# A weight ring of 24 parts instead of 23, two tiles' residual rows in PSUM, and the second tile's returned rows summed by GpSimd and VectorE

## The reference

```python
x  = x + token_mixer(rms_norm(x, norm_mix), ...)        # attention and gated linear attention
hn = rms_norm(x, norm_ffn)
g_logits = hn @ w_rg + b_rg                             # 4 groups: the best one
e_logits = hn @ w_re + b_re                             # 8 experts in a group: the best two
for each expert e:                                      # 32 experts, 1024 -> 256 -> 1024
    out += weight[:, e] * ((silu(hn @ w_gate[e]) * (hn @ w_up[e])) @ w_down[e])
return rms_norm(x + out, norm_final)
```

## Time and profile before

| | us |
|---|---|
| median of 3 runs | 604.9 (604.71 to 605.81) |
| the profiled execution | 604.58 |
| its span in the profile | 602.8 |
| TensorE busy | 574.2 (95%) |
| VectorE busy | 254.6 (42%) |
| ScalarE busy | 214.5 (36%) |
| GpSimd busy | 61.6 (10%) |
| mean of the DMAs | 259 GB/s |

### The profile page before, as it was taken

How to read it: one execution, slowest core, us unless ns; L and a number is a source line. 1 busy time by engine, 2 the same in 40 slices (tenths; PEclk the granted TensorE clock), 3 DMA queues, 4 the chain that set the end, 5 groups by cost and what they waited for, 6 DMA issues and landing times.

```text
span 602.8 us, 8673 instructions
## 1 busy us (share of the span) xinstructions
PE 574.2 (95%) x3428; PEld 434.6 (72%) x3429; DVE 254.6 (42%) x572; ACT 214.5 (36%) x438; POOL 61.6 (10%) x106
## 2 busy tenths in 40 slices
PE   7999999999999999999999998999999999877885
PEld 4978989888788888888888874766666676544342
DVE  4645677645445765533472375211211211101126
ACT  6634666555786522422152241011111111100114
POOL 3110000001000001100000011012211221111002
PEclk9999999999999999999999999999999999999898
DMA  8365130712231222198789667999999999999996
GB/s 301 87 207 177 58 111 5 291 59 71 71 104 46 61 70 71 37 342 280 291 310 414 246 252 276 380 414 425 422 421 425 424 424 421 425 425 423 425 385 277
DMA packets 59435, 156.02 MB, mean 259 GB/s; under 512 B 8368, under 2 KB 38472, under 8 KB 47744
## 3 DMA queue, kind: packets, MB, share of 16 engines
q1 hardware_dynamic: 54512, 145.74, 63.3%
q0 software_dynamic: 4864, 9.69, 4.2%
q10 hardware_dynamic: 16, 0.00, 0.0%
HBM read 147.31 MB, written 16.27 MB: 271 GB/s over the span
## 4 chain that ended last, share of the span: by engine, by line
PE 76%; DMA 11%; SPq 5%; DVE 4%; ACT 2%; issue 1%; POOL 1%; DVEq 0%; ACTq 0%; POOLq 0%
PE mid_rows L810 17%; PE last_rows L810 16%; PE bank L1247 12%; DMA slots<-expert_w_up 9%; PE bank L810 7%; PE bank L803 5%; SPq L555 5%; PE mid_rows L1267 5%; PE last_rows L868 2%; PE mid_rows L945 2%; DMA w<-w_in 1%; PE mid_rows L868 1%; PE bank L923 1%; PE bank L1118 1%; PE bank L924 1%
## 5 line engine op out<-in xcount | busy, mean ns | idle before, releaser
L1247 PE MATMUL bank<-slots,xgT 128*64 128x256 f32 x544 | 73.0, 381 | 5.2 <-DMA slot2b<-expert_w_up 1.9
L1882 DVE TENSOR_TENSOR w_low<-w,w_high 128x1024 fp32r<-128x1024 f32 x32 | 39.2, 1225 | 78.5 <-ACT w_high L1503 78.5
L1247 PEld LDWEIGHTS bank<-slots,xgT 128*64 128x64 f32 x544 | 49.2, 137 | 23.0 <-issue 4.0
L2237 DVE TENSOR_SCALAR y<-mid_rows,slot_weights 128x512 f32<-128x512 f32 x15 | 11.3, 751 | 99.7 <-PE mid_rows L1267 99.7
L1503 ACT ACTIVATE w_high<-w 128x1024 fp32r<-128x1024 f32 x32 | 33.7, 1054 | 48.6 <-PE last_rows L810 48.6
L1678 ACT ACTIVATE y<-mid_rows,slot_weights 128x512 f32<-128x512 f32 x15 | 10.3, 687 | 95.0 <-PE mid_rows L1267 70.8
L1247 PE MATMUL bank<-slot2b,xgT 128*64 128x256 f32 x240 | 36.6, 381 | 0.2 <-DMA slot2b<-expert_w_up 0.2
L1267 PE MATMUL mid_rows<-slots,hT 128*64 128x512 f32 x112 | 29.1, 594 | 2.6 <-issue 2.6
L1672 ACT ACTIVATE h_silu<-bank 128x256 f32<-128x256 f32 x15 | 5.8, 383 | 72.1 <-PE bank L1247 72.1
L1247 PEld LDWEIGHTS bank<-slot2b,xgT 128*64 128x64 f32 x240 | 23.7, 137 | 7.6 <-issue 1.6
L810 PE MATMUL mid_rows<-x_high,w_high 128*128 128x512 f32 x72 | 28.7, 398 | 0.0
(11 more groups left out here) (424 smaller groups left out, 1368.8 us busy)
## 6 DMA issues: line engine op xcount, KB each, us to landing
slots<-expert_w_up SPq DMA_DIRECT2D x18, 1024.0 KB, 24.3
slots<-expert_w_gate SPq DMA_DIRECT2D x17, 1024.0 KB, 12.8
slots<-expert_w_down SPq DMA_DIRECT2D x15, 1024.0 KB, 24.5
w<-w_in SPq DMA_DIRECT2D x16, 512.0 KB, 3.7
slot2b<-expert_w_up SPq DMA_DIRECT2D x8, 1024.0 KB, 27.2
slot2b<-expert_w_gate SPq DMA_DIRECT2D x7, 1024.0 KB, 16.7
w<-w_in SPq DMA_DIRECT2D x7, 840.0 KB, 4.6
slot2b<-expert_w_down SPq DMA_DIRECT2D x5, 1024.0 KB, 28.9
```

The source lines that it names most:

```text
L1247: ins = mm(bank[2][e * SLOTS:(e + 1) * SLOTS, m * FE:(m + 1) * FE], xgT[:, c, e * SLOTS:(e + 1) * SLOTS], weights(own, m, e, c * FE, (c + ...
L1882: V.tensor_tensor(wl2[:, u % 2, :], raw2[:, u % 2, :], wh2[:, u % 2, :].bitcast(F32), ALU.subtract).then_inc(s["lo_done"], 1)
L2237: V.tensor_scalar(y_sb[:, 512:1024], bank[5][:, :], weight, None, ALU.mult).then_inc(s["y_outD"], 1)
```

## The change

- **Ring.** R becomes 24. The old two-piece place becomes one whole place (`slot2f`, over tiles 2 and 3 of `x2`), and `split` now has three pieces: the front of `fixed` (4 KB), 2 KB beside the hidden activations and 2 KB in `early`. `early` is one allocation that holds constants and small tables that nobody needs once `act_done` is set. Part 23, the first that lies there, is issued after the halved parts (now 24 and 25) and after a wait for `act_done`. Four parts are loaded in three DMAs (before: four in two).
- **Room for it.** `h_silu` and `h_sb` become one buffer, multiplied in place; `slot_weights`, `by_pair` and `last_tokens` lie elsewhere.
- **PSUM.** Tile 2's rows stay in `mid_rows` from the residual to the end, as tile 3's do in `last_rows`. So nothing else may use banks 4 and 5: the turned rows of tiles 2 and 3 go to banks 0, 2 and 3, 0, the rank and count products to banks 2 and 3, and the down products to banks 0 and 1. `turn_x` writes these too and now waits for `y_outA` and `y_outD`. The last pair's gathered rows are turned into banks 2 and 3.
- **Tail.** ScalarE's copies of `x2` into `mid_rows` are gone. Tile 1's two returned rows are loaded beside each other, added by GpSimd, and the sum is added to `x2` by VectorE before the two accumulations of tile 1; TensorE's four products for them are gone. All eight products of the last pair now stand ahead of the returned rows' products.

```diff
-        TURNED = ((0, 1), (2, 3), (4, 5), (3, 5))
+        TURNED = ((0, 1), (2, 3), (0, 2), (3, 0))
-        LT_BANK = {0: 0, 2: 2, 3: 4}
+        LT_BANK = {0: 1, 2: 2, 3: 0}
-        split = (fixed[:, 0:PART // 2], place_at(YB + 3 * D, "slot2f", PART // 2)[:, :])
+        slot2f = place_at(YB + 2 * D, "slot2f", PART)
+        split = (fixed[:, 0:PART // 2], place_at(SMALL + 512, "slot2g", 512)[:, :], early[:, 0:512])
+        SPLIT_AT = (0, PART // 2, PART // 2 + 512, PART)
         ring = (part0 + [behind[4]] + part1 + [slot2a[:, i_ * PART:(i_ + 1) * PART] for i_ in range(2)]
-                + [behind[3]] + behind[0:3] + [slot2c[:, :], slot2d[:, :], slot2e[:, :], split])
+                + [behind[3]] + behind[0:3] + [slot2c[:, :], slot2d[:, :], slot2e[:, :], slot2f[:, :], split])
-        h_silu, h_sb = place_at(SMALL, "h_silu", FE)[:, :], place_at(SMALL + FE, "h_sb", FE)[:, :]
-        hT = v3(place_at(SMALL + 2 * FE, "hT", 2 * P), P)
+        h_silu = h_sb = place_at(SMALL, "h", FE)[:, :]
+        hT = v3(place_at(SMALL + FE, "hT", 2 * P), P)
         def rows_of(t):
-            return x2[:, t, :] if t < NT - 1 else last_rows[:, :]
-
-        def summed_rows(t):
             return (x2[:, 0, :], x2[:, 1, :], mid_rows[:, :], last_rows[:, :])[t]
...
                 if ring[q % R] is split:
-                    load_half(q, 0)
-                    load_half(q, 1)
+                    for i, piece in enumerate(split):
+                        cols = slice(SPLIT_AT[i], SPLIT_AT[i + 1])
+                        sp.dma_start(piece, (g_rows, u_rows, d_rows)[m][:, 2 * pair + e, cols]).then_inc(m_in[pair % 4][m], 16)
...
                 sp.wait_ge(s["g_done"], h + 1)
                 for e in range(2):
                     load_half(R + e, h)
+            sp.wait_ge(s["act_done"], 1)
+            load_part(23)
...
-                sp.dma_start(zt[:, t], rows.rearrange("(p w) n -> p w n", w=2) if t == 0 else
+                sp.dma_start(zt[:, t], rows.rearrange("(p w) n -> p w n", w=2) if t < 2 else
                              rows.rearrange("(i p) n -> p i n", i=2)).then_inc(s[f"rows_in{t}"], 16)
...
             pool.sem_inc(s["moe_done"], 1)
+            pool.wait_ge(s["rows_in1"], 32)
+            nc.gpsimd.tensor_tensor(zt[:, 1, 0, :], zt[:, 1, 0, :], zt[:, 1, 1, :], ALU.add).then_inc(s["row_sum"], 1)
...
             def turn_hn(t):
                 pe.wait_ge(s["hn_done"], t + 1)
                 for c in range(KC):
-                    if t == NT - 1 and c % 4 == 0:
-                        pe.wait_ge(s["hnT_outD"], 2 + c // 4)
+                    if t == 2 and c % 4 == 0:
+                        pe.wait_ge(s["hnT_outA"], 1 + c // 4)
+                    if t == 3 and c % 4 == 0:
+                        pe.wait_ge(s[("hnT_outD", "hnT_outA")[c // 4]], 2 + c // 4)
...
-            def turn_x(n, k, loads):
+            def turn_x(n, k, loads, rows_out):
                 pe.wait_ge(s[f"gathered{k}"], 16 * loads)
                 xv = xg[k].rearrange("p (q c) -> p c q", c=KC)
                 for c in range(KC):
+                    if rows_out is not None and c % 4 == 0:
+                        pe.wait_ge(s[("y_outA", "y_outD")[c // 4]], rows_out)
...
-                            ins = mm(bank[4 + f][e * SLOTS:(e + 1) * SLOTS, :], hT[:, j, e * SLOTS:(e + 1) * SLOTS],
+                            ins = mm(bank[f][e * SLOTS:(e + 1) * SLOTS, :], hT[:, j, e * SLOTS:(e + 1) * SLOTS],
...
             to_tokens(0, 0, 2, True).then_inc(s["comb_done"], 1)
-            to_tokens(0, 1, 3, True)
+            to_tokens(0, 1, 3, True).then_inc(s["comb_done"], 1)
+            to_tokens(0, 2, 4, False)
             to_tokens(0, 3, 6, False)
-            to_tokens(1, 0, 1, True).then_inc(s["comb_done"], 1)
-            to_tokens(1, 1, 0, True)
+            to_tokens(1, 0, 0, True).then_inc(s["comb_done"], 1)
+            to_tokens(1, 1, 1, True).then_inc(s["comb_done"], 1)
+            to_tokens(1, 2, 5, False)
             to_tokens(1, 3, 7, False)
-            pe.wait_ge(s["rows_in1"], 32)
-            rows_to_tokens(1, 0, 3).then_inc(s["comb_done"], 1)
-            rows_to_tokens(1, 1, 0).then_inc(s["comb_done"], 1)
-            for f in range(2):
-                pe.wait_ge(s["mid_in"], f + 1)
-                to_tokens(f, 2, 4 + f, False)
...
-            for f in range(2):
-                act.wait_ge(s["ly_lo"], f + 1)
-                A(mid_rows[:, f * 512:(f + 1) * 512], x2[:, 2, f * 512:(f + 1) * 512], ACT.Copy).then_inc(s["mid_in"], 1)
...
-                    V.tensor_tensor(x2[:, t, cols] if t < NT - 1 else bank[k][:, :], x2[:, t, cols], bank[k][:, :], ALU.add
+                    V.tensor_tensor(rows_of(t)[:, cols], x2[:, t, cols], bank[k][:, :], ALU.add
                                     ).then_inc(s["x2_done"], 1)
...
             accumulate(1, 0, 0, 2)
-            accumulate(2, 0, 1, 1)
-            accumulate(3, 1, 0, 3)
-            accumulate(4, 1, 1, 0)
+            accumulate(3, 0, 1, 0)
+            dve.wait_ge(s["row_sum"], 1)
+            dve.wait_ge(s["dve_step"], step(V.tensor_tensor(x2[:, 1, :], x2[:, 1, :], zt[:, 1, 0, :], ALU.add)))
+            accumulate(2, 1, 0, 3)
+            accumulate(4, 1, 1, 1)
```

More of the change, by code:

```diff
@@ L139, in hybrid_encoder, with early_view @@
         K = {n: cst[:, a:b] for n, (a, b) in CONST.items()}
-        rb = sb("rb", [P, NG + EXPERTS])
-        sink = sb("sink", [P, HEADS])
-        gcol = sb("gcol", [P, KC])
+        early, at_ = sb("early", [P, 540]), 0
+        def early_view(shape, words, dt=F32, rows=P):
+            nonlocal at_
+            at_ += words
+            view = early[0:rows, at_ - words:at_]
+            view = view if dt == F32 else view.bitcast(dt)
+            if len(shape) == 1:
+                return view
+            return view.rearrange("p (a b) -> p a b", b=shape[1]) if len(shape) == 2 else view
+        rb = early_view([NG + EXPERTS], NG + EXPERTS)
+        sink, gcol = early_view([HEADS], HEADS), early_view([KC], KC)
+        dec = early_view([GH, 2 * NT], 2 * GH * NT)
+        between = early_view([GH, NT - 1], GH * (NT - 1))
+        oss, ors = early_view([NT, GH], NT * GH), early_view([NT, GH], NT * GH)
+        selb = early_view([NT, EXPERTS], NT * EXPERTS // 2, BF16)
+        beforeb, onesb = early_view([P], P // 2, BF16), early_view([P], P // 2, BF16)
+        pi = early_view([5, 2 * NT], 10 * NT, I32)
+        cnt = early_view([EXPERTS + PAIRS], EXPERTS + PAIRS, F32, 1)
+        actf = early_view([116], 116, F32, 1)
+        assert 512 <= at_ <= 540
         row_norms = sb("row_norms", [P, 6, NT])
@@ L297, in hybrid_encoder @@
         ZERO_PIECES = 2 * NT
-        arrived = {(n_, m_): sum(32 if q_ in HALVED or ring[q_ % R] is split else 16 for q_, (p_, w_, _) in enumerate(order)
+        arrived = {(n_, m_): sum(16 * len(split) if ring[q_ % R] is split else 32 if q_ in HALVED else 16 for q_, (p_, w_, _) in enumerate(order)
                                  if w_ == m_ and p_ % 4 == n_ % 4 and p_ <= n_) for n_ in range(PAIRS) for m_ in range(3)}
@@ L429, in weights @@
                 return at[:, a:b]
-            return at[a // D][:, a % D:a % D + b - a]
+            piece = max(i for i in range(len(split)) if SPLIT_AT[i] <= a)
+            return at[piece][:, a - SPLIT_AT[piece]:b - SPLIT_AT[piece]]
         def down_rows(n, e, j, f):
@@ L567, in load_half @@
                 cols = slice(h * PART // 2, (h + 1) * PART // 2)
-                sp.dma_start(split[h] if ring[q % R] is split else ring[q % R][:, cols], (g_rows, u_rows, d_rows)[m][:, 2 * pair + e, cols]).then_inc(m_in[pair % 4][m], 16)
+                sp.dma_start(ring[q % R][:, cols], (g_rows, u_rows, d_rows)[m][:, 2 * pair + e, cols]).then_inc(m_in[pair % 4][m], 16)
             sp.wait_ge(s["lo_done"], LOWS)
@@ L1196, in _ @@
             for u in range(NT):
-                ins = mm(bank[4][0:1, P:P + EXPERTS], onesb[:, 0:1], selb[:, u, :], start=(u == 0), stop=(u == NT - 1),
+                ins = mm(bank[3][0:1, P:P + EXPERTS], onesb[:, 0:1], selb[:, u, :], start=(u == 0), stop=(u == NT - 1),
                          skip_group_check=True)
@@ L1831, in _ @@
             dve.wait_ge(s["const_in"], 32)
-            V.tensor_copy(beforeb[:], K["before"]).then_inc(s["cb_done"], 1)
-            V.tensor_copy(onesb[:], K["ones"]).then_inc(s["cb_done"], 1)
+            V.tensor_copy(beforeb, K["before"]).then_inc(s["cb_done"], 1)
+            V.tensor_copy(onesb, K["ones"]).then_inc(s["cb_done"], 1)
             V.tensor_copy(pair_base, K["e512"][0:1, :]).then_inc(s["cb_done"], 1)
@@ L2089, in router_out @@
                 V.tensor_tensor(lg[:, t0:t1, :], bank[1 + t0][:, t0 * (NG + EXPERTS):t1 * (NG + EXPERTS)].rearrange(
[L2090 removed]
+                    "p (t n) -> p t n", n=NG + EXPERTS), rb.unsqueeze(1).to_broadcast([P, t1 - t0, NG + EXPERTS]), ALU.add
                     ).then_inc(s["rl_out"], 1)
@@ L2161, in _ @@
```

(4 more changed lines are left out.)

62 lines of the change are left out of this document (27 added, 35 removed).

## The result

The changed kernel takes 611.65 us (median of 4, 611.41 to 612.97), the kernel before 605.07 in the same runs: a ratio of 1.0107 (95% interval 1.0089 to 1.0126). The profiled execution took 611.71 with a span of 609.9. It is slower, as forecast, but by 6.6 us instead of 3.0, and lies outside the forecast range of 604.7 to 608.9.

What follows compares the result with a forecast made beforehand. The prediction took the kernel as bound by weight DMAs, then a serial tail of 26 us. From a median of 604.9 us, 3.2 lost in the tail less 0.2 gained by the ring gave 607.9, range 604.7 to 608.9.

Steps and rivals of the forecast that it cites:

- Bound by the DMAs, then a serial tail: Expert stage: DMAs need 17.3 us a pair against TensorE's 12.0; then the last 26 us are serial.
- The ring of 24 parts: Weight prefetch, 380 to 382 us: a 24th place gains 0.2 us; ends 1.3 gained and 0.3 lost.
- The pieces, as a term of the same step: Four parts loaded in three pieces, half of each in 2 KB rows: at worst 0.3 us lost.
- Router and pair loop, nothing: Moved PSUM banks before and in the expert pairs: waits covered by 0.15 and 2.5 us, so no cost.
- The tail: After the last weights: GpSimd's 2.2 us sum delays VectorE's second addition; tile 1's squares start 3.2 us late.
- One sign: In the tail: tile 1's squares would start 2 to 3 us after tile 0's end, where they followed at once.
- the first (GpSimd misses the boundary): Tail: rows land 0.2 us later, GpSimd's sum follows VectorE's second addition; 1.9 us late, 606.6 us; chance 0.29.
- The second (no blocking): Tail: GpSimd's sum hardly delays VectorE, or takes only 1.1 us; 1.0 to 1.4 late, about 605.9; chance 0.12.
- The third (a gain of the ring): Weight prefetch: the 24th place gains 1.3 to 2.47 us; 603.4 to 604.9 us; chance 0.12.
- The fourth (the ring gives nothing, 608.1): Weight prefetch: part 23 loads too late, gaining 0, tail as forecast; 608.1 us, counted inside the main case.
- The sum: Whole kernel: 3.2 lost in the tail less 0.2 gained by the ring, added to 604.9: 607.9 us.
- the main case: Whole kernel: GpSimd's sum goes ahead of VectorE's second addition; 607.9 us, own range 606.9 to 608.9; chance 0.44.

Runs made afterwards that it cites:

- the pieces alone: Kernel before, with its four split parts loaded in three DMAs instead of two, the second half in two pieces with 2 KB rows: 605.80 us, ratio 1.0015.
- part 23 out of the way: Changed kernel with 32 bytes taken away and second tile's rows added by TensorE (605.87), part 23 issued behind part 29, 8 us later: 605.83 us, ratio 1.0007.
- where it was made to happen: Changed kernel with 32 bytes taken away (608.69), GpSimd's sum made to wait until both VectorE additions are done: 607.75 us, ratio 1.0033.

## Why the prediction was wrong, step by step

- **Bound by the DMAs, then a serial tail:** right. Both losses were read at exactly these two places.
- **The ring of 24 parts:** this step failed. The last up weights were to land within 0.5 us of where they did; they came 4.17 later. By medians the ring as built, with its addresses, lost 3.7 where 0.2 gained was the term. Its ends were 1.3 gained and 0.3 lost, and both took the rate behind 390 us as given ("the same 96 parts are loaded"). That rate fell by 1.4%, 3.0 us, because the places start 32 bytes off a multiple of 256. The new allocation stood in the diff, but no term was made for where the places come to lie.
- **The pieces, as a term of the same step:** 0.2 gained, with 0.3 lost as the end, was too hopeful. The ring with its pieces measured 0.7 lost, the pieces alone 0.65. The queue was never dry, as the step itself found, and then a place filled earlier gives nothing; I should have taken 0. SP's three issues took 1.90 us, not 1.3:

```profile
380.40 0.80 SPq L566 DMA_DIRECT2D fixed<-expert_w_gate  x1
381.25 0.66 SPq L566 DMA_DIRECT2D slot2g<-expert_w_gate  x1
381.95 0.44 SPq L566 DMA_DIRECT2D early<-expert_w_gate  x1
383.01 0.88 SPq L568 DMA_DIRECT2D slots<-expert_w_up  x2
```

The next refill was issued at 383.01 instead of 382.67; with part 23 out of the way it was issued at 382.93, and the kernel took as long (605.83).

- **Router and pair loop, nothing:** right as far as it can be seen. The first refill behind the router was issued at 374.38 in the changed kernel and at 374.06 with its 32 bytes taken away (before: 374.04; all other runs 373.8 to 374.3), which shows no clear loss.
- **The tail:** right in its mechanism. Predicted 3.2, by profile 3.18 (3.0 from the first addition on), by medians 2.8. GpSimd's sum took 2.2 us without its wait, as taken. It was let in at the boundary between the two additions, with 0.2 us of its 2.40 spent waiting, as forecast from the earlier trace rows. That it came in time was in part luck: rows and addition were both 4.3 us later than in the timeline forecast, and the margin was 0.2 us (0.5 in the kernel with the 32 bytes taken away). One sign was misnamed: tile 1's squares were to start 2 to 3 us after the end of tile 0's and started 1.07 after it; the prediction's own times, with tile 0's squares from 593.8 on, give about 1. Nor is TensorE's end set by the last rows' landing before the change, as it says: the products of tile 3's rows waited for no DMA there. Nothing in the sum hangs on either.
- **The rivals:** the first (GpSimd misses the boundary) did not happen; where it was made to happen it saved 0.9 us by medians and 0.7 by timelines, forecast 1.3. There the sum took 2.37 us instead of 2.2 and began 0.2 after the addition's end. The second (no blocking) is refuted by the 3.29 us. The third (a gain of the ring) found nothing in any kernel. The fourth (the ring gives nothing, 608.1) comes nearest for the ring, though its reason, a late `act_done`, did not occur: the first of the three pieces was issued at 380.40, about where it was forecast (380.12). A rival with a lower rate of all transfers was missing, and it is what carried the time beyond the range.
- **The sum:** 605.07 + 3.0 (addresses) + 2.8 (tail) + 0.7 (ring and pieces) = 611.6. Without the first term it is 608.6, and the kernel without it measured 608.69, in the main case's own range of 606.9 to 608.9. The lower end of the stated range should have been 604.6 by the prediction's own terms (604.9 - 1.3 + 1.0), not 604.7; it decides nothing.

No variant is faster than the kernel before: the nearest are at ratios of 1.0004 to 1.0014.

## What to carry to other kernels

When an edit adds, resizes or moves a small allocation, work out where the large DMA destinations behind it come to lie: in a stage bound by DMAs, here a start off a multiple of 256 bytes cost 1.2 to 1.4% of the rate over the whole stage (423 to 417 or 418 GB/s), with a full share that hides it, so compare GB/s and not shares. A sum moved to GpSimd isn't free beside VectorE operations with two SBUF operands: here they took turns, and the one on the critical path paid nearly the other's whole length (2.05 us for a sum of 2.2). A further prefetch place is worth only the time in which the queue is empty; the landing 7.0 us after its issue, behind a backlog, said here that there was none.

## What the runs showed of the hardware that was not expected

- The same loads, apart from the front of `fixed`, into places 0, 32, 64 and 128 bytes off a multiple of 256 ran at 423, 417, 418 and 418 GB/s (390 to 570 us), and the kernel took 605.19, 607.99, 607.75 and 607.63 us. A packet of 8 KB took 309.6, 314.3, 313.7 and 313.1 ns (400 to 560 us).
- Which two matrices were read in rows of 4 KB together went with the rate in 380 to 385 us: 320 GB/s (gate and down of different experts), 234 (two down, the same kernel otherwise) and 230 (down and up, in the ring of 24), at shares of 0.86 to 0.95. A packet of 4 KB took 189, 239 and 263 ns there. Each is one trace. Whether this is how the matrices lie in device memory wasn't tried.
- Cutting a piece with rows of 4 KB into two with rows of 2 KB cost 0.65 us by medians (0.2 to 1.6), though only four of 96 parts have such pieces.
